# Two key-page groups read and turned before attention starts, and one half weight panel split during the triangular inverse

## What is computed

```python
hcat = x @ w_in                                  # 1024 -> 3592 columns
q, k, v = l2/silu(causal_conv(hcat[..., :1536])) # gated DeltaNet, 4 heads of 128
o_dn, s = gated_delta_rule(q, k, v, g, beta, s0) # chunk form: needs inverse of (eye + lower)
o_dn = rms_norm(o_dn) * norm_w * silu(z)
o_mb = moba_attend(mq, k_all, v_all, pos0)       # samples: 2048 cached keys/values each, by page table
y = concat([o_dn, o_mb], -1) @ w_out             # 1024 x 1024
```

## Time and profile before

| | |
|---|---|
| median of 3 runs | 1147.16 us (1146.79 to 1147.16) |
| the profiled execution | 1148.01 us |
| its span, first to last instruction | 1146.0 us |
| PE busy | 1085.0 us (95%) |
| DVE busy | 705.4 us (62%) |
| ACT busy | 538.4 us (47%) |
| POOL busy | 298.2 us (26%) |
| DMA | 182.60 MB, mean 159 GB/s |
| mean granted TensorE clock | 0.983 |

### The profile page before, as it was taken

One profiled execution on the slowest core, in us unless ns is written; L12 is line 12 of the kernel. 1 busy time (PEld: TensorE's weight loads), 2 busy tenths in 40 slices (PEclk: granted clock), 3 DMA queues, 4 the chain that ended last, 5 costly groups with the idle time before them and its releaser, 6 DMA issues.

```text
span 1146.0 us, 20139 instructions
## 1 busy us (share of the span) xinstructions
PE 1085.0 (95%) x7047; PEld 978.0 (85%) x7047; DVE 705.4 (62%) x1187; ACT 538.4 (47%) x856; POOL 298.2 (26%) x285
## 2 busy tenths in 40 slices
PE   7999998888999998998999999999999899999996
PEld 6999888566666665598999999989999899999996
DVE  4853654678777777658666653475565866665344
ACT  3337621257666666545444433253334644443324
POOL 8400144203777777233000000132004400000111
PEclk9999988889999999999999999999999999999999
DMA  7344200368999896542444443425435344444321
GB/s 217 137 144 153 74 1 1 119 208 288 324 299 305 303 307 220 190 147 92 152 153 152 154 155 121 162 74 153 149 145 154 102 151 153 152 155 150 124 87 46
DMA packets 120882, 182.60 MB, mean 159 GB/s; under 512 B 6224, under 2 KB 61615, under 8 KB 120750
## 3 DMA queue, kind: packets, MB, share of 16 engines
q1 hardware_dynamic: 118402, 174.61, 46.0%
q0 software_dynamic: 2416, 7.16, 2.1%
HBM read 176.12 MB, written 5.63 MB: 159 GB/s over the span
## 4 chain that ended last, share of the span: by engine, by line
PE 80%; DVE 12%; issue 3%; ACT 3%; DMA 1%; SPq 0%; DVEq 0%; ACTq 0%
PE bank L1758 74%; PE bank L2106 4%; DVE kTl L1176 2%; DVE lo L1169 2%; ACT hi L765 1%; DMA xtok<-x_sample 1%; DVE xres L1609 1%; DVE sbias L1483 1%; DVE gs L1479 1%; DVE sbias L1474 1%; DVE xl L1616 1%; DVE xres L1176 0%; PE bank L2332 0%; PE bank L2237 0%; PE bank L1777 0%
## 5 line engine op out<-in xcount | busy, mean ns | idle before, releaser
L1758 PE MATMUL bank<-xh,hi 128*128 128x320 f32 x1184 | 369.8, 312 | 10.1 <-DVE xl L1616 5.1
L1758 PE MATMUL bank<-xl,hi 128*128 128x320 f32 x1184 | 367.1, 310 | 0.0
L1758 PE MATMUL bank<-xh,lo 128*128 128x320 f32 x1184 | 366.9, 310 | 0.0
L1169 DVE TENSOR_TENSOR lo<-raw,hi 128x2048 fp32r<-128x2048 f32 x102 | 240.8, 2361 | 185.7 <-ACT hi L765 185.7
L765 ACT ACTIVATE hi<-raw 128x2048 fp32r (+2 forms) x124 | 217.9, 1758 | 117.3 <-PE bank L1758 116.0
L1758 PEld LDWEIGHTS bank<-xh,hi 128*128 128x128 f32 x1184 | 223.3, 189 | 15.3 <-issue 7.2
L1758 PEld LDWEIGHTS bank<-xl,hi 128*128 128x128 f32 x1184 | 223.4, 189 | 0.1
L1758 PEld LDWEIGHTS bank<-xh,lo 128*128 128x128 f32 x1184 | 223.4, 189 | 0.0
L1758 PE MATMUL bank<-hh,hi 128*128 128x320 f32 x416 | 128.9, 310 | 1.3 <-DVE hraw L1176 1.3
L1758 PE MATMUL bank<-hh,lo 128*128 128x320 f32 x416 | 128.3, 308 | 0.0
L1758 PE MATMUL bank<-hl,hi 128*128 128x320 f32 x416 | 128.3, 308 | 0.0
(11 more groups left out here) (405 smaller groups left out, 1561.8 us busy)
## 6 DMA issues: line engine op xcount, KB each, us to landing
raw<-w_up SPq DMA_DIRECT2D x44, 1024.0 KB
kring<-cache_k SPq DMA_DIRECT2D x88, 256.0 KB, 3.8
vring<-cache_v SPq DMA_DIRECT2D x84, 256.0 KB, 4.9
raw<-w_down SPq DMA_DIRECT2D x8, 2048.0 KB
raw<-w_in_mix SPq DMA_DIRECT2D x6, 2048.0 KB
raw<-cache_v SPq DMA_DIRECT2D x44, 256.0 KB, 4.9
raw<-cache_k SPq DMA_DIRECT2D x40, 256.0 KB, 3.5
raw<-w_in_sc SPq DMA_DIRECT2D x8, 1024.0 KB
```

The source lines that it names most:

```text
L1169: dve.tensor_tensor(lo[:, p], weight(n)[:, :, 256 * p:256 * p + 256], hi[:, p], ALU.subtract)\
L1758: return pe.matmul(out, lhsT, rhs, start=start, stop=stop, **kw)
```

## The change

The diff, cut to its core. The first two key groups get pages of their own (`kfirst`, over the memory of `xh` and `xl`); SP loads them when the input projection has ended. The ring starts with group 2 and takes over the waits that groups 0 to 2 had. On PE the first two transposes stand before `sample_state(3)` and `o_sums((0, 1))`, and the wait for `rowc` behind these. On DVE `add_state(3)` stands behind `kT_lo(1)`; on ACT `o_logs((0, 1))` behind `kT_hi(0)`, `kT_hi(1)` and the two queries; on POOL the store of state 3 behind the queries. The second `vnm` buffer moves into slot 7's weights, of which `lo[:, 0]` must by then have been made: `split_lo(S_OUT, 0)` is moved from unit 11 of the last sequence to the place behind level 4 of tile 1 in the inverse. The step lists and the semaphores `k_first0` and `k_first1` follow suit.

```diff
+        kfirst = sb("kfirst", [P, 2 * KD * TOK], stack=sX)
...
-        vnm = [tP[0:SMP, :, :].rearrange("p a c -> p (a c)"), sc0[0:SMP, 1024:2048]]
+        vnm = [tP[0:SMP, :, :].rearrange("p a (e v) -> p (a e) v", v=HD),
+               raw[0:SMP, KD * 512:2 * KD * 512].rearrange("p (k c) -> p k c", c=512)[:, :, 0:HD]]
...
+        first_pages = [kfirst[:, at:at + 2048].rearrange("p (j c) -> p j c", c=512) for at in (2560, 512)]
...
                 if n == 0:
+                    sp_.wait_ge(s["chunk_done"], 4 * SLOT_MIX + CREDIT)
+                if n < 2:
+                    load_pair(first_pages[n][:, 0:2], a["cache_k"][0], f"k_first{n}", 2 * n)
+                    load_pair(first_pages[n][:, 2:4], a["cache_k"][0], f"k_first{n}", 2 * n + 1)
+                if n == 2:
                     PE.wait(sp_, "o1")
                     DV.wait(sp_, "qg1")
-                if n == 1:
+                if n == 3:
                     PE.wait(sp_, "stS2")
-                if n == 2:
+                if n == 4:
                     sp_.wait_ge(s["stores"], 16 * 7)
-                if n < 4 * NB:
-                    after(sp_, "kT_mm", 4 * (n - KS) + 4)
+                if 2 <= n < 4 * NB:
+                    if n >= 2 + KS:
+                        sp_.wait_ge(s["kT_mm"], 4 * (n - KS) + 4)
+                    at = (n - 2) % KS
...
-            for h in range(H):
+            for h in range(H - 1):
+                store_state(h)
...
                 queries_lo(b)
+            store_state(H - 1)
...
-            o_logs((0, 1))
+            kT_hi(0)
+            kT_hi(1)
             queries(0)
             queries(1)
-            kT_hi(0)
-            kT_hi(1)
+            o_logs((0, 1))
...
             for n in range(2, len(INV)):
                 inverse(n)
+                if INV[n] == (4, 1):
+                    split_lo(S_OUT, 0)
...
             add_state(2)
-            add_state(3)
...
+            DV.wait(dve, "stS2")
             dve.memset(qp[:, :, :].bitcast(F32), 0.0)
...
             kT_lo(0)
             kT_lo(1)
+            add_state(3)
...
-                    if (b, u) == (NB - 1, 11):
-                        split_lo(S_OUT, 0)
...
             sample_state(2)
-            sample_state(3)
...
-            o_sums((0, 1))
...
                 if stage == "kv0":
                     AC.wait(pe, "oln3")
+                    DV.wait(pe, "stS3")
...
-            AC.wait(pe, "vnsb1")
-            AC.wait(pe, "oT1")
-            DV.wait(pe, "rowc")
...
+            AC.wait(pe, "vnsb1")
+            AC.wait(pe, "oT1")
             transpose(0)
             transpose(1)
+            sample_state(3)
+            o_sums((0, 1))
+            DV.wait(pe, "rowc")
```

More of the change, by code:

```diff
@@ L66 @@
 SEMS = """
-params_in xleft_in xtok_in first_in y_out hist_in wba_in pt_in raw_in k_in0 k_in1 k_in2 v_in0 v_in1 v_in2 v_in3 v_in4 v_in5 s0_in0 stores
+k_first0 k_first1 params_in xleft_in xtok_in first_in y_out hist_in wba_in pt_in raw_in k_in0 k_in1 k_in2 v_in0 v_in1 v_in2 v_in3 v_in4 v_in5 s0_in0 stores
 hi_done lo_done chunk_done rel_act conv_step
@@ L121 @@
 spread inv10 inv11 inv12 inv13 inv14 inv15 inv16 vnm0 state0 rhsa1 rhs1 vnm1 oT2 stS0 vnm2 statea state1 stS1 vnm3
-stS2 stS3 rowc0 foldb rowc on10 on11 mixo0 mixo1 mixl0 mixl1 plog0 pmaxa0 pmax0 plog1 pmaxa1 pmax1 prec0 pnorm0 prec1
+stS2 rowc0 foldb rowc stS3 on10 on11 mixo0 mixo1 mixl0 mixl1 plog0 pmaxa0 pmax0 plog1 pmaxa1 pmax1 prec0 pnorm0 prec1
 pnorm1 pol0 pol1 vol r0_0 r0_1 r0_2 r0_3 r0_4 r0_5 r0_6 r0_7 mean0 vara0 var0 centred0 t2_0_0 t2_0_1 xl0_0 t2_0_2
@@ L160, in trunk_program @@
         lo = sb("lo", [P, 2, KD, 256], F32R)
+        sX = ExitStack()
+        kfirst = sb("kfirst", [P, 2 * KD * TOK], stack=sX)
+        sX.close()
         xh = sb("xh", [P, KD, TOK], F32R)
@@ L450, in _ @@
                 if n == 0:
+                    sp_.wait_ge(s["chunk_done"], 4 * SLOT_MIX + CREDIT)
[3 more added lines that the diff above has]
+                if n == 2:
                     PE.wait(sp_, "o1")
                     DV.wait(sp_, "qg1")
-                if n == 1:
+                if n == 3:
                     PE.wait(sp_, "stS2")
-                if n == 2:
+                if n == 4:
                     sp_.wait_ge(s["stores"], 16 * 7)
-                if n < 4 * NB:
-                    after(sp_, "kT_mm", 4 * (n - KS) + 4)
-                    k = kpages[n % KS]
-                    load_pair(k[:, 0:2], a["cache_k"][0], f"k_in{n % KS}", 2 * n)
-                    load_pair(k[:, 2:4], a["cache_k"][0], f"k_in{n % KS}", 2 * n + 1)
+                if 2 <= n < 4 * NB:
+                    if n >= 2 + KS:
+                        sp_.wait_ge(s["kT_mm"], 4 * (n - KS) + 4)
+                    at = (n - 2) % KS
+                    load_pair(kpages[at][:, 0:2], a["cache_k"][0], f"k_in{at}", 2 * n)
+                    load_pair(kpages[at][:, 2:4], a["cache_k"][0], f"k_in{at}", 2 * n + 1)
                 if n == V_LAG // 2 + 1:
@@ L635, in _, with store_state @@
             pool.dma_start(o["dn_p"][0, 0].rearrange("h d v -> d h v"), t4(spr[:, :])).then_inc(s["stores"], 16)
-            for h in range(H):
+            def store_state(h):
                 DV.wait(pool, f"stS{h}")
@@ L1353, in apart @@
                     PE.wait(dve, f"stS{h - 2}")
-                DV.up(tt(vnm[h % 2].rearrange("p (b v) -> p b v", v=HD), mid(vnewS[:, 128 * h:128 * h + 128], NB),
+                DV.up(tt(vnm[h % 2], mid(vnewS[:, 128 * h:128 * h + 128], NB),
                          last(member, HD), ALU.mult), f"vnm{h}")
@@ L2010, in sample_state @@
                 bk = 4 if h % 2 else 6
-                mm(bank[bk][:, :], ktok[0:SMP, 2, P * h:P * h + P], vnm[h % 2][:, 0:512])
-                PE.up(mm(bank[bk + 1][:, :], ktok[0:SMP, 2, P * h:P * h + P], vnm[h % 2][:, 512:1024]), f"stS{h}")
+                mm(bank[bk][:, :], ktok[0:SMP, 2, P * h:P * h + P], vnm[h % 2][:, 0:4, :])
+                PE.up(mm(bank[bk + 1][:, :], ktok[0:SMP, 2, P * h:P * h + P], vnm[h % 2][:, 4:8, :]), f"stS{h}")
             DV.wait(pe, f"inv{INV.index((6, 0))}")
@@ L2102, in transpose @@
                 if h == 0:
-                    pe.wait_ge(s[f"k_in{g % KS}"], 64 * (g // KS + 1))
+                    if g < 2:
+                        pe.wait_ge(s[f"k_first{g}"], 64)
+                    else:
+                        pe.wait_ge(s[f"k_in{(g - 2) % KS}"], 64 * ((g - 2) // KS + 1))
                 after(pe, "kT_lo", n - 2)
+                pages = first_pages[g] if g < 2 else kpages[(g - 2) % KS]
                 for j in range(4):
-                    ins = pe.transpose(bank[n % 3][:, P * j:P * j + P], kpages[g % KS][:, j, P * h:P * h + P], ident[:, :])
+                    ins = pe.transpose(bank[n % 3][:, P * j:P * j + P], pages[:, j, P * h:P * h + P], ident[:, :])
                 ins.then_inc(s["kT_mm"], 1)
```

## The result

| | before | after |
|---|---|---|
| median of the runs, us | 1147.16 (6 runs, 1146.19 to 1150.97) | 1141.24 (6 runs, 1138.39 to 1141.67) |
| ratio of the runs | 1 | 0.9937, 95% interval 0.9923 to 0.9951 |
| the profiled execution, us | 1148.01 | 1138.39 |
| its span, us | 1146.0 | 1136.4 |
| mean granted clock in it | 0.983 | 0.986 |

A forecast was written before the change was run, and what follows sets the result against it. The prediction saw a hole between DeltaNet and attention, with waits through DVE's clearing there and its subtraction near attention's end. Terms 4.2 + 0 + 1.9 = 6.1 us, from 1147.16 to 1141.1; range 1139.0 to 1144.5.

The forecast's parts named there:

- handover: Between DeltaNet and attention: the new order on PE, ACT and DVE gains 4.2 us, bounds 3.9 and 5.9.
- inverse: Behind level 4: the moved subtraction fits DVE's wait of 3.10 us and costs 0; without that cover 2.3 us.
- end: End of attention: without the subtraction, PE's wait of 1.93 us goes; gain 1.9 us, bounds 1.0 and 3.3.
- The clearing: DVE's clearing of `qp` in the handover begins at 223.6 us, 3.4 us earlier, with `add_state(3)` out of its way.
- `kT_hi(3)`: ACT in the handover: starts at 230.5 us instead of 235.16, 4.6 us earlier, with the table load counted.
- the upper end of 5.9: Handover gain if ACT's 1.28 us table load for the logarithm lay under other work: 5.9 us.
- The 0.4 us given back by `keyb`: DVE in the handover: `keyb` between `kT_lo(2)` and `kT_lo(3)` gives back up to 0.7 us; 0.4 taken.
- the reading of the earlier trace: DVE's subtraction beside POOL waits for the one operation in flight, and POOL's next operation waits for DVE.
- The 0.2 us of lateness: In the inverse, the moved subtraction ends at 198.43 us, 0.2 us late; PE has some 0.3 us in hand.
- Rival 3: Inverse: POOL keeps the port for four scalings, level 5 is 7.6 us late; 1151.7 us, slower by 4.5; chance 0.04.
- Rival 1: Handover: the clock falls all the same, so the gain is 3.4 to 4.7 us, 1142.5 to 1143.8; chance 0.18.
- Rival 2: First attention units: the new order or a late DVE port loses about 2 us; 1143.3 to 1145.0; chance 0.12.

The follow-up runs named there:

- e3: Changed kernel with the subtraction put back at the end of attention, so only the handover is changed; mean 1140.26 us, ratio to before 0.9937.
- e2: Kernel before with only the subtraction for the output panel moved into the inverse; mean 1146.66 us, ratio to before 0.9989 (0.9976 to 1.0003).
- e6: Changed kernel with one ACT table set for logarithm and exponential in place of two separate loads; mean 1139.24 us, ratio to before 0.9924.
- e9: Changed kernel with a second subtraction of the same size, result unused, ahead of the moved one in the inverse; mean 1146.76 us, ratio to before 0.9992.
- e4: Changed kernel with the first two key transposes on PE behind sample_state(3), leaving PE's hole open; mean 1143.42 us, ratio to before 0.9956.
- e5: Kernel before with eight unused transposes of a constant tile in PE's hole before sample_state(3); mean 1144.53 us, ratio to before 0.9971.
- e8: Changed kernel with one table set for logarithm and exponential and the copies into spread behind the inverse; mean 1135.66 us over 12 runs, a repeat included.
- e10: Repeat of the changed kernel with one table set and the copies into spread behind the inverse; mean 1135.66 us over the 12 runs of both measurements.
- e7: Changed kernel with DVE's eight small copies into spread moved from the middle of the inverse to behind it; mean 1140.32 us, ratio to before 0.9927.

## Why the prediction was right

- **The place of the gain.** Taken: handover 4.2 us (3.9 to 5.9), inverse 0, end 1.9 (1.0 to 3.3), sum 6.1. Measured inside one execution: 4.74, 0.00 and 1.83 to 1.87, sum 6.6. e3 and e2 give the first and the last term each with its own edit.
- **The clearing** was to be 3.4 us earlier: from the first mark it was 19.95 us before (227.05 - 207.10) and is 16.65 after, 3.30 earlier.
- **`kT_hi(3)`** was to be 4.6 us earlier with the table load on the chain. It was 28.06 us behind the first mark (235.16 - 207.10) and is 23.32: 4.74 earlier. The table load is on the chain; e6 took it off and got 1.15 us at this mark, close to the 1.28 that the upper end of 5.9 rested on.
- **The 0.4 us given back by `keyb`** was wrong: the handover distance shrinks by the full 4.74. `keyb` (226.40, 1.10 us) does come between two `kT_lo`, as said. But ACT is then in its second table load (227.26 to 228.54), which the sum had left out, and the next `kT_hi` waits for that, not for DVE. One delay hid the other: e6, without the load of 1.28 us, gains only 0.54 us in this place.
- **The inverse.** Both sides of the reading of the earlier trace rows held: DVE waited for POOL's operation in flight and came next (3.21 us against 3.2 said, POOL 9.51 against 9.8), and the next level was not late. The 0.2 us of lateness that was said did not show. The margin was thinner than zero cost makes it look: e9 shows that the next subtraction costs 4.7 us. Rival 3 (POOL keeps the port for all four) did not happen in any of the ten profiles with the subtraction in the inverse. The Trainium skill (SBUF — State Buffer, Who interferes with whom) describes the contention of the two engines over their shared ports as an exclusive lock. The trace agrees: the subtraction took 3.21 us where it takes 2.29 alone, and POOL's first scaling 3.94 us where the others took 1.89.
- **Rival 1, the clock.** It did not fall: 1.00 from 217 to 232 us, in all profiles of the changed kernel. The Trainium skill (TensorE: Matmul & The Clock Gate, Part 4: PE-mode transpose) says that transposes do not count as PE-busy in the same way and that the full clock does not engage for them. By that rule the handover would have gained 1.4 to 2.7 us less. The traces speak against it for these fp32 transposes, and e4 and e5 do so from both sides: without them in the hole 3.44 us for `sample_state(3)`, with them 1.98, whether they are of use or not. A filled hole is no guarantee, though: in e8 the clock fell all the same.
- **Rival 2, given back later,** did not happen in attention, where it was looked for: the attention distance shrinks by just what e2 alone takes from it. But 1.2 us is given back behind the third mark, in all three profiles of the changed kernel (680.1 us to the end where it was 679.0). The prediction had no term for what lies there.
- **The total.** That the median is off by 0.1 us is luck. The terms measured 6.6 us and not 6.1, and 1.2 of it was lost again behind the third mark, which leaves 5.4; over all runs the difference is 7.5 ± 0.6; and a single kernel's median of six moves by a microsecond. So some 2 us of the 7.5 lie in places that no term covers. The mean clock rose by 0.0042, which over a span of 1146 us is 9.6 us less of the low level. That is close to the 10.2 us of the handover, but only the profiled executions show where the low time lies. The clock's falls elsewhere come and go by themselves: in the step of the table's last column it fell in the profiles of before, e2 and e4, in part in e3 and e9, and not in the others, and the difference of the two profiled executions (9.6 us) has 2.55 us of it. Whether such a fall is chance or hangs on something in the programs was not settled.

## What to carry to other kernels

A hole of 2 us on PE ahead of thin work can cost as much again in the work behind it (1.2 us in e5, up to 2.2 in e4): put work into it whose inputs can be in memory early, and look at the granted clock behind it, not only at the wait. Moving a step into another engine's wait is free up to the length of that wait and dear beyond it, so measure the cover with the neighbour's contention included (3.2 us here, not 2.3). And where the runs spread by 5 us, judge an edit of 2 us by the distance between two marks in one execution, check that the clock is low in the same places between them, look behind the last mark too, and look for table loads and small copies that stand between them.

## What the runs showed of the hardware that was not expected

- Transposes that compute nothing shorten what follows: in e5 eight of them (1.09 us) turn 3.16 us of matmuls into 1.98 and 2.50 into 1.34. In e8, with eight useful ones in the same place, the second group of matmuls took 2.15 all the same.
- The clock falls in different places in different executions of one program. In the three profiles of the changed kernel the low time is 31.3, 28.0 and 38.2 us over the whole span, of which 17.1, 13.7 and 17.1 lie between 100 and 500 us; e8 has a fall at 218.7 us that e10, the same program, doesn't have.
- A copy of 32x4 elements took 1.10 us beside an operation of POOL, where its like took 0.16; in e7, elsewhere, the first of them took 0.54 and the others at most 0.16. A small copy was not small beside a busy POOL.
- Two long operations queued on both DVE and POOL take turns: 3.22 and 3.98 us for DVE's two, 11.55 for POOL's four (7.46 alone).
